# Hybrid decoder step on one core: last requests' tail moved under the pages, samples in column groups to the router, a shorter choice of experts

## The reference

```
x = x + concat(o_da, o_hg) @ w_out            # 1024 x 1024
h = rmsnorm(x, norm2_w)
pg = softmax(h @ wg + bg)                      # 4 groups
p_top, g = top_k(pg, 1)
le = (h @ we + be).reshape(-1, 4, 4)[g]        # 4 experts of the chosen group
top_l, e = top_k(le, 2)
gate = p_top * softmax(top_l)
x = x + sum over the two experts of gate * (silu(h @ w1[e]) * (h @ w3[e])) @ w2[e]
y = rmsnorm(x, final_norm_w)
```

## Time and profile before

| what | value |
|---|---|
| median of three runs | 1461.84 us (1460.27 to 1467.7) |
| profiled execution, its span | 1460.45 us, 1458.6 us |
| TensorE busy | 1269.8 us (87%), 9162 matmul records |
| VectorE busy | 629.8 us (43%) |
| ScalarE busy | 371.9 us (25%) |
| GpSimd busy | 111.4 us (8%) |
| last product of the last prompt quarter ends | 1105.6 us |
| first product of the experts begins | 1161.3 us |
| first product of the final combination with gathered rows | 1410.1 us |

### The profile page before, as it was taken

The page is one execution under the profiler, slowest core; times in us unless marked ns, Lnnn a source line. Parts: engine busy times, 40 slices in busy tenths (PEclk is TensorE's granted clock), DMA queues, the critical chain, the costliest instruction groups (busy, mean ns, idle before and its releaser), DMA issues.

```text
span 1458.6 us, 24015 instructions
## 1 busy us (share of the span) xinstructions
PE 1269.8 (87%) x9162; PEld 894.6 (61%) x9162; DVE 629.8 (43%) x1498; ACT 371.9 (25%) x745; POOL 111.4 (8%) x272
## 2 busy tenths in 40 slices
PE   0899998989998899988787876999996499999975
PEld 0566786767667788665464644555554387878741
DVE  0400323445355556456857673475516412121216
ACT  3411200121222224335544642132122011111112
POOL 0500000000000001020000000000000111111030
PEclk9899999999999999999888997999997599999998
DMA  7531101001020106567887879999850599999654
GB/s 208 200 117 51 58 29 44 30 18 43 1 89 1 60 1 218 179 247 259 305 280 253 307 244 363 331 361 359 303 196 31 188 316 296 305 300 306 211 222 185
DMA packets 163717, 274.02 MB, mean 188 GB/s; under 512 B 19041, under 2 KB 78178, under 8 KB 163618
## 3 DMA queue, kind: packets, MB, share of 16 engines
q1 hardware_dynamic: 141072, 221.90, 44.9%
q0 software_dynamic: 11104, 38.28, 7.3%
q10 hardware_dynamic: 11442, 12.51, 2.8%
HBM read 235.55 MB, written 37.09 MB: 187 GB/s over the span
## 4 chain that ended last, share of the span: by engine, by line
PE 68%; DVE 14%; ACT 4%; SPq 4%; issue 4%; DMA 3%; ACTq 2%; POOL 0%; DVEq 0%; POOLq 0%
PE bank L1048 16%; PE bank L1051 13%; PE bank L1434 10%; PE bank L1325 5%; DVE arena L1705 5%; PE bank L1454 4%; PE bank L1091 3%; PE bank L1211 2%; PE bank L1170 2%; SPq L550 2%; SPq L548 2%; DMA arena<-in_cache_k_dram 1%; ACTq L716 1%; PE bank L1449 1%; PE bank L1255 1%
## 5 line engine op out<-in xcount | busy, mean ns | idle before, releaser
L1048 PE MATMUL bank<-arena 128*128 128x352 f32 x768 | 239.1, 470 | 0.0
L1048 PEld LDWEIGHTS bank<-arena 128*128 128x128 f32 x768 | 147.5, 195 | 81.0 <-issue 6.7
L1051 PE MATMUL bank<-arena 128*128 128x256 f32 (+1 forms) x864 | 195.4, 384 | 0.6 <-issue 0.6
L1051 PEld LDWEIGHTS bank<-arena 128*128 128x128 f32 (+1 forms) x864 | 154.9, 182 | 33.1 <-issue 5.7
L1705 DVE STREAM_TRANSPOSE arena<-arena 128x512 f32<-128x512 f32 x256 | 155.9, 675 | 21.7 <-DMA arena<-in_cache_k_dram 21.3
L1434 PEld LDWEIGHTS bank<-arena 128*128 128x128 f32 x1024 | 142.4, 192 | 9.2 <-issue 9.2
L1434 PE MATMUL bank<-arena 128*128 128x160 f32 x1024 | 143.5, 301 | 1.9 <-DVE arena L2010 1.9
L1325 PE MATMUL bank<-arena 128*128 128x512 f32 x256 | 120.2, 613 | 7.7 <-DMA arena<-in_w_out_dram 7.7
L1170 PE MATMUL bank<-arena,tab 128*32 128x256 f32 x1024 | 71.1, 425 | 17.8 <-ACT arena L817 11.8
L1325 PEld LDWEIGHTS bank<-arena 128*128 128x128 f32 x256 | 47.0, 194 | 61.6 <-issue 53.4
L757 ACT ACTIVATE arena<-bank 128x352 f32<-128x352 f32 x48 | 22.3, 464 | 225.8 <-PE bank L1048 225.8
(11 more groups left out here) (302 smaller groups left out, 1468.4 us busy)
## 6 DMA issues: line engine op xcount, KB each, us to landing
arena<-in_cache_k_dram SPq DMA_DIRECT2D x256, 256.0 KB, 4.9
arena<-in_cache_v_dram SPq DMA_DIRECT2D x256, 256.0 KB, 3.8
arena<-in_expert_w_dram SPq DMA_DIRECT2D x48, 1024.0 KB, 7.3
arena<-in_w_in_dram SPq DMA_DIRECT2D x14, 1024.0 KB, 5.1
expert_scratch<-route POOLq DMA_DIRECT2D x40, 256.0 KB, 5.7
expert_scratch<-arena ACTq DMA_DIRECT2D x16, 512.0 KB
out_dram<-arena SPq DMA_DIRECT2D x12, 512.0 KB, 2.7
arena<-in_x_prompt_dram SPq DMA_DIRECT2D x4, 1024.0 KB, 11.0
```

The source lines that it names most:

```text
L1048: mm = nc.tensor.matmul(bank(g)[:, 0:N3], w[:, k, c * P:(c + 1) * P], hT[:, k * TOK + n * N3:k * TOK + (n + 1) * N3], start=(k == 0), stop ...
L1051: mm = nc.tensor.matmul(bank(g)[0:ROWS[c], 0:256], tok(hT, k, c), w[:, k, :], start=(k == 0), stop=(k == KC - 1))
```

## The change

It does these things:

- The 56 beats are spread over 30 quarters instead of 28, so that they end at `(7, 1)`.
- Requests 0 to 6 are divided, combined, squared and copied inside the quarters `(6, 2)` to `(7, 3)`. The last request is scaled by ScalarE in `keep_output`, combined by a product of its own behind `mixed_out(7, 2)`, and its sum of squares is taken by ScalarE. `sample_out(0)` moves from behind the last quarter to behind `(7, 2)`, that is ahead of `mixed_out(7, 3)`. The scaling by `daw` is one instruction instead of four.
- The samples stay in the 4 column groups (128 partitions x 256 columns, `x1c`): one addition instead of four, a square of 256 columns, four small products (`sample_square`, with a constant table that folds the four groups) for the sum over the groups, a flip of two transposes instead of eight, and a router that picks its 32 columns out of them. Rows are stored by a DMA that puts the groups back. In the final combination four products through the identity bring the groups back to 32 rows.
- The four loads of the samples' x move from behind the last page to ahead of the eight prompt rows of x, ahead of the pages of request 5.
- The router's weights get four more columns, of zeros, with a bias of -3e38, so that the 8 first logits need no copy. GpSimd clears them at the start, and two of ScalarE's loads wait for it.
- `choose` makes the mask in one instruction (not equal, times -1e30) and adds it, without the product; the one-hots are made by instructions that take a number for each partition, the second together with the sum. `rk` is gone: two products of 16 columns over the last tile's `c3` and `M3` give the counts, ahead of the two of 144.
- In the final combination, `residual(i + 2)` stands behind `diag(i)` for i from 2 and waits for `combine(i - 2)`.

```diff
-        w_beat = [min(BEATS, u_beat[-1] + -(-(BEATS - u_beat[-1]) * (k + 1) // 28)) for k in range(len(quarters))]
+        w_beat = [min(BEATS, u_beat[-1] + -(-(BEATS - u_beat[-1]) * (k + 1) // 30)) for k in range(len(quarters))]
...
+                    for c in range(4):
+                        sp.dma_start(x_smp[32 * c:32 * c + 32, :], xs_v[:, c * 256:c * 256 + 256]).then_inc(sem("x1_in"), 16)
                     for i in range(8):
                         sp.dma_start(x1[i], xp_v[:, i, :]).then_inc(sem("x1_in" if i < 2 else "x1_more"), 16)
...
+            nc.gpsimd.memset(rbias[:, NG:NG + 4], -3e38).then_inc(sem("wr_pad"), 1)
+            nc.gpsimd.memset(wr[:, :], 0.0).then_inc(sem("wr_pad"), 1)
...
+                if b == NB - 1:
+                    act.wait_ge(sem("d_step"), 1)
+                nc.scalar.activation(o_all[:, b * P:(b + 1) * P], ps[7][:, 0:P], ACT.Copy, scale=rsum[:, b:b + 1] if b == NB - 1 else 1.0).then_inc(sem("o_kept_d"), 1)
...
+                if (i, q) == (7, 1):
+                    act.wait_ge(sem("d_step"), 2)
+                    nc.scalar.activation(osq[0:16, 0:7 * P], o16[0:16, 0:7 * P], ACT.Square).then_inc(sem("d_act"), 1)
                 decode(w_spot[(i, q)])
+                if (i, q) == (7, 2):
+                    act.wait_ge(sem("d_ps"), 3)
+                    nc.scalar.activation(osq[0:16, 7 * P:8 * P], ps[7][0:16, P:2 * P], ACT.Square, accum_out=oms[0:16, 7:8]).then_inc(sem("d_act"), 1)
+                if (i, q) == (7, 3):
+                    act.wait_ge(sem("d_step"), 3)
+                    nc.scalar.activation(orms[0:16, :], oms[0:16, :], ACT.Sqrt).then_inc(sem("d_act"), 1)
...
-                if i == 7 and q == 0:
+                if (i, q) == (6, 2):
...
-                if i == 7 and q == 2:
+                if (i, q) == (7, 0):
                     pe.wait_ge(sem("d_step"), 1)
...
+                if (i, q) == (7, 2):
+                    pe.wait_ge(sem("o_kept_d"), NB)
+                    nc.tensor.matmul(ps[7][0:16, P:2 * P], comb, o_all[:, 7 * P:8 * P], start=True, stop=True).then_inc(sem("d_ps"), 1)
+                    pe.wait_ge(sem("d_step"), 2)
+                    sample_out(0)
             pe.wait_ge(sem("d_step"), 4)
...
             pe.wait_ge(sem("routing"), ROUTING["counts"])
+            nc.tensor.matmul(ps[6][:, 64:80], ones, cum[:, 8 * NE:9 * NE], start=True, stop=False)
+            nc.tensor.matmul(ps[6][:, 64:80], ones, Mx[:, 8 * NE:9 * NE], start=False, stop=True).then_inc(sem("routing_ps"), 1)
...
+                if i == 8:
+                    for c in range(4):
+                        mm = nc.tensor.matmul(ps[c // 2][0:SMP, c % 2 * 256:c % 2 * 256 + 256], ident[:, 32 * c:32 * c + 32], x1c, start=False, stop=(c % 2 == 1))
                 mm.then_inc(sem("x1_ps"), 1)
-                if i + 4 < TILES:
-                    pe.wait_ge(sem("x1_ready"), 20 + i + 1)
-                    residual(i + 4)
+                if 2 <= i < TILES - 2:
+                    pe.wait_ge(sem("x1_ready"), 17 + i - 1)
+                    if i + 2 < 8:
+                        residual(i + 2)
...
-                for c in range(4):
-                    part = slice(32 * c, 32 * c + 32)
-                    V.tensor_tensor(x1[8][0:32, c * 256:(c + 1) * 256], ps[5][part, 0:256], x_smp[part, :], ALU.add).then_inc(sem("x1_ready"), 1)
+                V.tensor_tensor(x1c, ps[5][:, 0:256], x_smp, ALU.add).then_inc(sem("x1_ready"), 1)
...
-                step(V.tensor_copy(head3(gpad, 8)[:, i, 0:NG], lg3[:, i, 0:NG]))
...
-                step(V.tensor_tensor(ohg[:, i, :], cst("iota")[:, 0:NG], gidx[:, i:i + 1].broadcast_to([P, NG]), ALU.is_equal))
-                ch.step(V.tensor_scalar(off[:, i, :], ohg[:, i, :], -NEG, NEG, ALU.mult, ALU.add))
+                step(V.tensor_scalar(off[:, i, :], cst("iota")[:, 0:NG], gidx[:, i:i + 1], NEG, ALU.not_equal, ALU.mult))
```

237 lines of the change are left out of this document (129 added, 108 removed).

## The result

The changed kernel took 1446.46 us in the median of four runs (1441.12 to 1448.35), the kernel before 1463.79 us in four runs beside it: a ratio of 0.988, 95% interval 0.9844 to 0.9916. That is 17.3 us, where 17.8 had been forecast (1444 against 1461.84). A later comparison gave 0.988 again (0.9862 to 0.9898). The sum behind the forecast was less right than its end.

A forecast was written before the change was run, and what follows sets the result against it. TensorE was taken as the bound, except in two serial chains, behind the last quarter and in the final combination. 1460.45 - 6.4 - 10.6 + 0.3 = 1443.8, said as 1444 us; 8 in 10 range 1438 to 1451.

The forecast's parts named there:

- The end behind the last quarter: Last quarter's end to VectorE's counts: 19.8 us instead of 28.1, so 8.3 us go; bounds 6.6 to 9.0.
- T: The end of the last prompt quarter; the forecast writes later times as T + x us.
- `sample_out(0)` among the quarters: Ahead of mixed_out(7, 3), where TensorE has no gap: it moves the last quarter's end by its 1.93 us.
- The requests inside the quarters: TensorE's four new waits in the quarters cost nothing, being covered by work queued in front of them.
- Beats: Spreading the beats over 30 quarters changes TensorE's waits for key transposes by 0, bounds -2.7 and +2.7 us.
- the rival of low clock and keys: Slow products behind the last quarter (+1.7), doubled transpose waits (+2.7), late loads (+1.75): 1450 us; chance 0.13.
- The combination: Final combination: reordered identity products save 11.6 us, less 1 for stores delaying gathers: 10.6, bounds 7.9 to 11.6.
- the first place: Behind the last quarter: 8.3 us saved less 1.9 for sample_out(0), net 6.4 us, bounds 4.7 to 7.1.
- that gathers bind: Rival for the final combination: stores delay each gather in full, 3.7 instead of 1 us, giving 1447 us; chance 0.14.
- The late loads: Samples' loads put 1.75 us of issuing ahead of x loads and pages; taken as 0, bound +1.75 us.
- The stop of the queue's head: Rival: TensorE stands between the last quarters because the scaling chain is late, and the clock falls: 1469 us; chance 0.04.
- a combination without effect: Rival: combine did not hold TensorE in the final combination, so only 6 us go: 1454 us; chance 0.04.

The follow-up runs named there:

- the kernel with held stores: Changed kernel with SP's nine result stores held until the combination's last gather has landed; 1448.95 us, ratio 0.991 to the kernel before.
- with 28: Changed kernel with the beats spread over 28 quarters again instead of 30; 1446.5 us, ratio 0.9878 to the kernel before.
- the useless products: Changed kernel with three useless 512-column TensorE products between the samples' sum of squares and tile 7's router; 1446.36 us; together with 28 quarters 1446.4 us.
- the half put back: Changed kernel with sample_out(0) moved back behind the last quarter, directly behind the router of tile 6; 1449.31 us, ratio 0.9914 to the kernel before.
- all three: Changed kernel with 28 quarters, sample_out(0) behind the last quarter and three useless products; 1442.8 us; with four more useless products ahead of residual(3), 1444.35 us.
- the combination alone: Kernel before with only the final combination's order changed, tile i+2's identity product behind tile i's diagonal; 1449.33 us, ratio 0.9901.

## Why the prediction came out, step by step

**The end behind the last quarter: the right chain, one term too small.** Over the traces with the code unaltered there, the counts began at (28.09 + 28.65 + 27.39) / 3 = 28.0 us before and (22.65 + 22.22 + 22.90 + 22.95) / 4 = 22.7 after (22.90 is the kernel with held stores). So 5.4 us went, not 8.3, and 22.7 lies outside the bounds of 19.1 to 21.5. The step that failed is "It fell behind 1112, over 6 us after T, so I take the fast value here: T + 4.9". Up to the start of `sample_out(4)` the times fit (2.8 us behind T, 3.0 forecast). Then this half took 3.36 instead of 1.93 and the router 3.61 instead of 2.61: 2.4 of the 2.85 us by which the first trace is late. The other 0.4 lie in the two small products before the counts (1.1 us with the handing over, 0.8 forecast) and in small rests. The end of the high clock had been taken as a point in time behind T. It depends on what TensorE does. By the clock records of the traces, the granted clock fell 7.3 to 8.6 us behind T in the three traces with the old end; 2.7 to 3.6 us behind it, at the start of `sample_out(4)` or under it, in all six with 30 and the half inside; at 8.7 with 28 and at 11.5 with the useless products besides; at 12.5 with the half put back; at 13.3 and 14.3 with all three. 28 and the half put back each give `sample_out(4)` its 1.93 us back; the useless products alone give the router 1.97 us and leave the half slow. With 28 and the useless products together the counts came at 19.75, the T + 19.8 of the forecast. So the new places of two pieces, the last beats in (7, 0) and (7, 1) and the half ahead of (7, 3), together took the clock from the half behind them, and the return of either gives it back. The tiny transposes and the wait of 0.5 us just behind T are not enough to explain it, since they stand there with 28 as well. Why beats some 10 us ahead of T should matter was not tried further; it stays open.

The Trainium skill, "TensorE: Matmul & The Clock Gate", Part 1, says that the default is the throttled clock and activity releases it. The runs agree that work keeps it: three useless products brought the router from 3.61 to 1.97 us. From this rule the prediction concluded that the sum would be at the good end of both bounds. The end behind the last quarter came out beyond the bad one (22.7 against 21.5): that the quarters are dense did not carry the clock past T.

**`sample_out(0)` among the quarters: its cost was right, its effect on the clock was missed.** The forecast cost was 1.93 us. The means of the quarters with it inside and behind are 201.9 and 199.8 with 30, 199.8 and 198.0 with 28 ((199.89 + 199.65) / 2 and (198.09 + 197.87) / 2): 2.0 and 1.8 us, where all means but the first rest on one or two traces. "Before it was free behind T" holds for the changed order only in part. Put back there with 30, it did not delay the counts, but there the clock had come back with it. Where the clock was high in either place (28 and useless products), the counts moved from 19.75 to 21.71 and 21.23, as much as the quarters lost.

**The requests inside the quarters: right.** The four waits cost nothing, TensorE 26.20 of 26.20 us. The only wait left is 0.5 us for the scaled transposes, behind T.

**Beats: 0 was taken.** 30 against 28 in the changed kernel is about +2, inside the bounds of 2.7 on either side, by TensorE's waits for keys, as the rival of low clock and keys had named them; the second trace of the changed kernel shows none of it. Against the kernel before, the quarters grew by 2.5 us in the mean (201.7 in the four traces with the code unaltered there, 199.2 in three before), which is the half and only some 0.5 more. So something else in the new quarters gave back about 1.5; it is not the shorter choice (201.71 with the old one), and what it is stays open. The start was right to 0.3: ScalarE's first held load began at 2.01 instead of 1.77 us, and the next stood where it had stood (3.34 and 3.30).

**The combination: right.** Forecast 10.6, bounds 7.9 to 11.6. The first trace gives 52.34 - 41.49 = 10.85. Over all traces of this order except the two that change the stores or the clock there, nine of them, the mean is 42.6 (41.0 to 43.7), so 52.2 - 42.6 = 9.6. The allowance of 1 us for stores fits the packets of the gathers, which end 0.7 to 1.0 us sooner with the stores held than in the two traces of the changed kernel; the wait of 1.08 us at tile 7 stands in two of the nine traces only. But the first three diagonals were not held by the clock alone, as the sum had it: behind the slow first one stood the gathers. The rule of the Trainium skill, "DMA: Bandwidth & Descriptors", in its section on queues, that a DMA engine goes round between the queues, gave a delay of at most the stores' 3.7 us. The traces stay within it: from before to after the slowest landing grew by 1.3 us in the first traces (8.8 to 10.1) and 2.3 in the second (7.7 to 10.0). How the engines take turns is shown by no run here.

**The sum.** Forecast: 6.4 + 10.6 - 0.3 = 16.7 us. By the stretches: quarters and end together (227.3 - 224.4) = 2.9, combination 9.6, and 0.3 in the two between: 12.8. The net term of the first place came to less than half (6.4 forecast, 2.9 measured), by 2.9 us at the end and 0.6 in the quarters. The ratios say 17.3 and 18.5 us in the medians, and the combination alone 14.5 (9.8 to 19.1 by the interval) where its trace shows 9.4. Each is higher than what the traces hold, and the traced executions of before, 1460.45 us in the first, lie under their medians of 1462 to 1466. The traced executions themselves are 15.4 us apart in the first pair and 11.3 in the second. The kernel before against itself moved by 3 us. So 4.5 to 5.7 us of the measured gain have no place in a stretch; whether they are spread between executions, or lie ahead of the quarters in untraced executions, stays open. The forecast of 1444 us is therefore right in its size with help from that remainder.

The rivals: that gathers bind is in part true (10.1 us of landing, 2.3 us of waits that came back), at a price within the forecast. Of low clock and keys the first half came true, at 2.4 us where 1.7 had been its price; the keys cost about 2 us against 28, but the quarters in all only 0.5 us more than the half. The late loads are neither shown nor excluded by the starts of the quarters. The stop of the queue's head and a combination without effect are excluded by the windows.

## What to carry to other kernels

Where TensorE walks hand in hand with another engine, let it have one more stage between its wait and the release: two lines put in another order were worth 9 to 10 us here, three quarters of what the traces show of the whole change. When you shorten a chain with TensorE in it, ask what will keep its clock up: a piece of its own work that is moved out of a wait costs its full length in the dense place, and may take the clock of what follows with it. Before you compare a minimum, a median and a maximum of two traces, look how many instructions of each they cover. Check the sum stretch by stretch against more than one trace; a total that agrees can hide a term that is off by more than half.

## What the runs showed of the hardware

- The granted clock fell while TensorE was busy for 4.50 of 5 us (0.74), in a stretch of a 24-column router, 16-row transposes, a wait of 0.5 us and `sample_out(4)`. With 28 quarters the same work behind T kept the high clock (1.93 us for `sample_out(4)`), so what stands there does not decide alone. In the kernel with `sample_out(0)` behind the last quarter 1.00 held over 5.00 of 5 and then over 3.26 of 5 us.
- On VectorE, a step on 4 or 16 columns that takes a number for each partition took 230 and 235 ns, one with two tensors on 16 columns 176 ns. A step saved by such a form saves less than a step: three steps fewer in `choose` took 3.16 us to 2.81, where the prediction had 2.65.
- Of eighteen gathers of half a megabyte, one issued every 1.24 us, the first landed after 4.5 to 5.5 us and the slowest after 7.7 and 8.8 in the old order and 9.0 to 10.1 in the new, whose stores start earlier (two and four traces that tell all 18), at 409 to 419 GB/s for all transfers together between 1410 and 1425 us of the changed kernel. Holding all stores back ended the gathers' packets only 0.3 to 1.2 us sooner than in the ten traces with the new order and free stores.
